# A two-layer encoder on one core: retention core interleaved with its out-projection, attention loop rebuilt, first norm as columns

## The reference, cut to what matters

```python
c_act = jax.nn.silu(c)
for i in range(DEPTH):                     # DEPTH = 2
    mod = c_act @ ada_w + ada_b            # 1024 x 6144
    sh1, sc1, g1, sh2, sc2, g2 = jnp.split(mod, 6, axis=-1)
    h = modulate(rmsnorm(x, n1), sh1, sc1) # h * (1 + scale) + shift
    m = retention_mixer(h, ...) if i == 0 else gqa_mixer(h, ...)
    x = x + g1[:, None, :] * m
    h = modulate(rmsnorm(x, n2), sh2, sc2)
    f = swiglu(h, ...) if i == 0 else moe_swiglu(h, ...)
    x = x + g2[:, None, :] * f
return modulate(rmsnorm(x, final_norm_g), fsh, fsc)

# retention: 4 heads, q and k 256 wide, v and gate 512 wide, w_in 1024 x 6144, w_out 2048 x 1024
y = (fwd + bwd)                            # decayed scores, forward and backward
y = ((y - mu) * lax.rsqrt(var + NORM_EPS)).reshape(bsz, seq, RET_V) * gn_g
return (jax.nn.silu(g) * y) @ w_out
# attention: 8 query heads, 2 key heads of 128, both RMS-normalised and rotated, softmax over 256 keys
# FFN: 2816 wide. Experts: 8, each 3584 wide, top 2 of 8 by token
```

## Time and profile before

| what | us |
|---|---|
| median of three executions | 1642.29 |
| profiled execution | 1642.87 |
| its span in the profile | 1641.0 |
| TensorE (PE) busy | 1545.9 |
| VectorE (DVE) busy | 1341.8 |
| ScalarE (ACT) busy | 976.7 |
| retention w_in, from unit 3 | 58.0 to 185.9 |
| retention core | 185.9 to 241.2 |
| its out-projection | 241.2 to 290.6 |
| FFN | 296 to 502 |
| QKV and attention | 509 to 620 |
| experts, last norm | 630 to the end |

### The profile page before, as it was taken

One profiled execution on the slowest core, in us unless ns is written; L12 is line 12 of the kernel. 1 busy time (PEld: TensorE's weight loads), 2 busy tenths in 40 slices (PEclk: granted clock), 3 DMA queues, 4 the chain that ended last, 5 costly groups with the idle time before them and its releaser, 6 DMA issues.

```text
span 1641.0 us, 20506 instructions
## 1 busy us (share of the span) xinstructions
PE 1545.9 (94%) x6782; PEld 1234.3 (75%) x6782; DVE 1341.8 (82%) x1047; ACT 976.7 (60%) x791; POOL 198.3 (12%) x189
## 2 busy tenths in 40 slices
PE   5999779899997779999999999999999999999996
PEld 4777547677776568888888888888888888888784
DVE  6799578877778668888888888888888888888897
ACT  3444523443334536677777677777777777777664
POOL 0399500000002001100100100000000000000600
PEclk8999979999998899999999999999999999999998
DMA  9799309688894417999999999999999999999992
GB/s 340 279 346 351 134 15 360 229 303 298 267 321 154 146 52 262 364 365 352 380 368 362 370 370 355 381 368 352 381 368 353 378 368 354 376 371 353 386 363 117
DMA packets 239918, 509.15 MB, mean 310 GB/s; under 512 B 16392, under 2 KB 39048, under 8 KB 239754
## 3 DMA queue, kind: packets, MB, share of 16 engines
q1 hardware_dynamic: 234704, 491.50, 83.0%
q0 software_dynamic: 4592, 15.08, 2.7%
q10 hardware_dynamic: 586, 2.11, 0.3%
HBM read 502.64 MB, written 7.87 MB: 311 GB/s over the span
## 4 chain that ended last, share of the span: by engine, by line
PE 89%; DVE 6%; ACT 1%; DMA 1%; issue 1%; SPq 0%; DVEq 0%; ACTq 0%
PE bank L1713 27%; PE bank L1714 27%; PE bank L1715 27%; PE bank L2045 1%; PE bank L1694 1%; PE bank L1803 1%; DVE lo L1096 1%; DMA xs<-in_x 1%; DMA stage<-in_l_moe_w_up 1%; PE bank L1708 1%; DVE hs L1134 0%; PE bank L1921 0%; DVE lo L1496 0%; SPq L453 0%; PE bank L2039 0%
## 5 line engine op out<-in xcount | busy, mean ns | idle before, releaser
L1496 DVE TENSOR_TENSOR lo<-stage,hi 128x2048 fp32r<-128x2048 f32 x168 | 386.3, 2306 | 52.4 <-ACT hi L958 51.8
L958 ACT CAST hi<-stage 128x2048 fp32r<-128x2048 f32 x168 | 321.4, 1913 | 118.2 <-DMA stage<-in_l_moe_w_up 94.2
L1714 PE MATMUL bank<-lo,hg_hi 128*128 128x512 f32 x896 | 354.6, 396 | 0.0
L677 ACT CAST hi<-stage 128x2048 fp32r<-128x2048 f32 x75 | 143.2, 1912 | 147.1 <-PE bank L1715 78.8
L1096 DVE TENSOR_TENSOR lo<-stage,hi 128x2048 fp32r<-128x2048 f32 x75 | 173.2, 2312 | 40.8 <-ACT hi L677 34.4
L1714 PEld LDWEIGHTS bank<-lo,hg_hi 128*128 128x128 f32 x896 | 168.9, 188 | 37.8
L1713 PE MATMUL bank<-hi,hT_hi 128*128 128x512 f32 x416 | 172.9, 416 | 9.9 <-DVE lo L1096 8.5
L1713 PE MATMUL bank<-hi,hg_hi 128*128 128x512 f32 x452 | 179.6, 397 | 1.4 <-DVE lo L1496 1.2
L1496 DVE TENSOR_TENSOR lo<-stage,hi_h 128x2048 fp32r<-128x2048 f32 x56 | 128.3, 2292 | 63.8 <-ACT hi_h L958 63.8
L1715 PE MATMUL bank<-hi,hg_lo 128*128 128x512 f32 x452 | 179.1, 396 | 0.0
L1714 PE MATMUL bank<-lo,eaT_hi 128*128 128x512 f32 x448 | 177.8, 397 | 0.0
(11 more groups left out here) (313 smaller groups left out, 2753.5 us busy)
## 6 DMA issues: line engine op xcount, KB each, us to landing
stage<-in_l_moe_w_gate SPq DMA_DIRECT2D x224, 512.0 KB, 4.6
stage<-in_l_moe_w_up SPq DMA_DIRECT2D x224, 512.0 KB, 5.2
stage<-in_l_moe_w_down SPq DMA_DIRECT2D x224, 512.0 KB, 4.8
ada_w<-in_l_ada_w SPq DMA_DIRECT2D x40, 1024.0 KB, 5.3
stage<-in_l_ret_w_in SPq DMA_DIRECT2D x48, 512.0 KB, 7.0
stage<-in_l_ffn_w_gate SPq DMA_DIRECT2D x22, 512.0 KB, 7.5
stage<-in_l_ffn_w_up SPq DMA_DIRECT2D x22, 512.0 KB, 8.6
stage<-in_l_ffn_w_down SPq DMA_DIRECT2D x22, 512.0 KB, 7.6
```

Of the source, the lines that this page charges most:

```text
L677: nc.scalar.copy(hi[:, b % HRING, :], stage[:, b % RING, :]).then_inc(hi_done, 1)
L958: nc.scalar.copy(hi_e(b), stage[:, b % RING, :]).then_inc(hi_done, 1)
L1496: nc.vector.tensor_tensor(lo[:, b % RING, :], stage[:, b % RING, :], hi_e(b).bitcast(F32), ALU.subtract).then_inc(lo_done, 1)
L1714: mm(dst_ap, a_hi, w_lo, start=False, stop=False)
```

## The change

It consists of three parts and a rotation of the cast buffers in the experts.

**First norm as columns.** c, the first norm's gain and the 2D bias values come packed as columns in one small DMA (`vecs`). x lands first; ScalarE scales it by the reciprocal root (`xr`), TensorE transposes it at once (`turn_x`, 16 transposes). `sum_pre` makes eight matmuls of one column, so shift and scale come out with channels on partitions; three small operations (`columns_pre`) finish them, and hT_hi, hT_lo are made per k of 128 channels (`high_pre`, `full_pre`, `low_pre`). The products of units 0 and 3 wait per k.

**Retention.** The decay arguments of all four heads are computed on VectorE at unit 8 of w_in, and the exponentials on ScalarE at unit 10. Ada halves 2 to 15 follow `low(u)` for u from 9 to 22 on VectorE; SyncE's text for w_in is unchanged. Gates go through Silu straight from PSUM. Head 0's transposes stand before the last unit of w_in. Heads and half units of the out-projection alternate; the out-projection's units come in another order, and so do the final ada halves.

**Attention.** The ada blocks leave it: `A_AT` is still loaded in the QKV projection but worked off, with `A_AT + 1`, in chunks 2 to 5 of the first expert. The rotation runs over two heads at a time; the transposes of the last queries, and their squares and roots, stand inside the head loop. The four output units are cast into other buffers (`high_o`).

Core of the diff:

```diff
-    sp.dma_start(ccol[:, :], c.rearrange("a (k p) -> p (a k)", p=P), allow_slow_non_contiguous=True).then_inc(c_in, 16)
+    sp.dma_start(vecs[:, :, :], columns.rearrange("p (a k) -> p a k", k=KT)).then_inc(c_in, 16)
+    xv = x.rearrange("a (t p) d -> p (a t) d", p=P)
+    for t in range(TT):
+        sp.dma_start(xs[:, t, :], xv[:, t, :]).then_inc(x_in[t], 16)
+    load_pre(0, 0)
     sp.dma_start(cst[:, 0:C_TRI], consts[:, 0:C_TRI]).then_inc(const_in, 16)
-    xv = x.rearrange("a (t p) d -> p (a t) d", p=P)
-    for k in range(KT):
+    for k in range(1, KT):
         load_pre(0, k)
-    sp.dma_start(xs[:, :, :], xv).then_inc(x_in, 16)
     load_in(0)
-    for u, ks in ((1, range(0, 4)), (2, range(4, 6)), (3, range(6, 8))):
+    load_in(1)
+    for u, ks in ((2, range(0, 2)), (3, range(2, 8))):
         for k in ks:
             load_pre(1, k)
         load_in(u)
...
         if 6 <= u < 6 + 2 * A_IN:
             a = u - 6
             load_ada(a // 2, a % 2, l0_ada_w, l0_ada_b, 2 * D + (a // 2) * AC)
-    for k in range(8):
-        n, kg = k // 4, k % 4
+    def load_out(k):
+        n, kg = OUT_ORDER[k]
         load(U_ROUT + k, w_out_v[:, 4 * kg:4 * kg + 4, n * CB:(n + 1) * CB])
-        load_ada(A_FIN + k // 2, k % 2, final_ada_w, final_ada_b, (k // 2) * AC)
...
+    def load_fin(i):
...
+        load_ada(A_FIN + i // 2, i % 2, final_ada_w, final_ada_b, (i // 2) * AC)
+    load_out(0)
+    load_fin(0)
+    load_out(1)
+    load_fin(1)
+    for k in range(2, 6):
+        load_out(k)
+    load_fin(2)
+    load_fin(3)
+    load_out(6)
+    load_fin(4)
+    load_out(7)
+    load_fin(5)
     load_pair(U_FF, 0, slice(0, FCH))
+    load_fin(6)
     load_pair(U_FF + 1, 4, slice(0, FCH))
+    load_fin(7)
...
+    chunks(0, 0, 1, 4)
+    load_ada(A_AT + 1, 0, l1_ada_w, l1_ada_b, (A_AT + 1 - A_L1) * AC)
+    chunks(0, 0, 4, 5)
+    load_ada(A_AT + 1, 1, l1_ada_w, l1_ada_b, (A_AT + 1 - A_L1) * AC)
+    chunks(0, 0, 5, N_EC)
...
     high_pre(1)
-    for u in range(5, 2 * N_IN + 3):
+    for u in range(4, 2 * N_IN + 1):
         cc = u // 2 - 2 if u >= 10 else u - 6
-        if u == 2 * N_IN + 2:
-            take_chunk(N_IN - 1)
         high(U_RET + u)
-        if 6 <= u < 9 or 10 <= u < 2 * N_IN + 2 and u % 2 == 0:
+        if 6 <= u < 9 or 10 <= u and u % 2 == 0:
             take_chunk(cc)
-        if u >= 11 and u % 2:
-            c = (u - 11) // 2
+        if u == 11:
+            ada_take(0, mod_at(2 * D))
+        if u >= 14 and u % 2 == 0:
+            c = (u - 12) // 2
             ada_take(c, mod_at(2 * D + c * AC))
...
+    qkv_copy(0)
+    qkv_squares(0)
+    high(U_QKV + 4)
     head_roots(0)
-    ada_take(A_AT, mod_at((A_AT - A_L1) * AC))
-    high(U_QKV + 4)
     high(U_QKV + 5)
-    qkv_take(1)
+    high_o(0)
+    high_o(1)
+    qkv_copy(1)
     aq_take(0)
-    high(U_AOUT)
+    qkv_squares(1)
+    aq_take(1)
+    act.wait_ge(w_used, RING + U_QKV + 4)
+    high_o(2)
     head_roots(1)
-    aq_take(1)
     aq_take(2)
-    high(U_AOUT + 1)
-    qkv_take(2)
-    head_roots(2)
     soft(0)
     soft(1)
-    aq_take(3)
-    aq_take(4)
+    act.wait_ge(w_used, RING + U_QKV + 5)
+    high_o(3)
+    qkv_copy(2)
     for h in range(AH):
         pT_take(h)
+        if h in (1, 3):
+            aq_take(3 + h // 2)
         if h:
             o_take(h - 1)
+        if h == 0:
+            qkv_squares(2)
+        if h == 1:
+            head_roots(2)
...
+    def columns_pre(half):
+        b, ks = COL_BANK[half], slice(AK * half, AK * half + AK)
+        dve.wait_ge(p_sum, half + 1)
+        nc.vector.tensor_tensor(pm[:, 0, ks], bank[:, b, 0:AK], vecs[:, 2, ks], ALU.add)
+        link(nc.vector.scalar_tensor_tensor(out=pm[:, 2, ks], in0=bank[:, b, AK:2 * AK], scalar=1.0,
+                                            in1=vecs[:, 3, ks], op0=ALU.add, op1=ALU.add))
+        nc.vector.tensor_tensor(pm[:, 1, ks], pm[:, 2, ks], vecs[:, 1, ks], ALU.mult).then_inc(p_col, 1)
+        dve.wait_ge(p_col, half + 1)
...
+        dve.wait_ge(xT_out, 4)
+        j = AK * half + k
+        link(nc.vector.tensor_scalar(yT[:, k, :], (xT0, xT1)[half][:, k, :], pm[:, 1, j:j + 1], pm[:, 0, j:j + 1], ALU.mult, ALU.add))
+    def low_pre(half, k):
+        j = AK * half + k
+        dve.wait_ge(h0_hi, j + 1)
+        nc.vector.tensor_tensor(hT_lo[:, j, :], yT[:, k, :], hT_hi[:, j, :].bitcast(F32),
...
-    low_pre(0)
+    pre(0, range(0, 1))
+    for t in range(TT):
+        dve.wait_ge(root_done, t + 1)
+        ins = nc.vector.reciprocal(rstd[:, t:t + 1], root[:, t:t + 1])
+        ins.then_inc(p_rstd, 1)
+    pre(0, range(1, KT))
+    columns_pre(0)
+    full_pre(0, 0)
+    full_pre(0, 1)
     low(U_RET)
-    pre(1, range(0, 4))
+    low_pre(0, 0)
+    low_pre(0, 1)
+    for k in (2, 3):
+        full_pre(0, k)
+        low_pre(0, k)
     low(U_RET + 1)
-    pre(1, range(4, 6))
+    pre(1, range(0, 2))
     low(U_RET + 2)
-    pre(1, range(6, 8))
-    low(U_RET + 3)
-    norm_pre(1)
-    low_pre(1)
-    low(U_RET + 4)
-    low(U_RET + 5)
+    pre(1, range(2, 8))
+    columns_pre(1)
+    for k in range(AK):
+        full_pre(1, k)
+        low_pre(1, k)
+    for u in range(3, 6):
+        low(U_RET + u)
...
     for u in range(6, 2 * N_IN):
         low(U_RET + u)
-        if u < 6 + 2 * A_IN:
-            ada((u - 6) // 2, u % 2)
...
+    weight(0)
+    stats(0)
+    weight(1)
+    gates(0)
+    stats(1)
+    low_y(0)
+    low_y(1)
+    weight(2)
+    gates(1)
+    stats(2)
+    low(U_ROUT + 2)
+    low_y(2)
+    low_y(3)
+    weight(3)
+    gates(2)
+    stats(3)
+    low_y(4)
+    low_y(5)
+    gates(3)
+    low(U_ROUT + 3)
+    fin(2)
+    low(U_ROUT + 4)
+    low_y(6)
+    low_y(7)
+    fin(3)
+    fin(4)
+    low(U_ROUT + 5)
+    fin(5)
...
-    link(head_rope(0))
...
     head_scales(0)
     kx = qkv[:, :, AH * AHD:(AH + AKV) * AHD].rearrange("p t (h d) -> p t h d", h=AKV)
...
-    low(U_QKV + 4)
     low(U_QKV + 5)
-    head_rope(1).then_inc(arope, 1)
+    head_rope(0, 2, qtab, 2 * TT).then_inc(arope, 1)
+    head_rope(2, 2, qtab, 2 * TT).then_inc(arope, 1)
     head_sums(1)
-    low(U_AOUT)
+    low_o(0)
     head_scales(1)
-    low(U_AOUT + 1)
...
+    for j in range(2, N_EC - 1):
+        b, i = U_MOE - 2 + 6 * j, 4 * (j - 2)
+        low_e(b)
+        ada_step(i)
+        e_mul(j - 1, RING + b - 2)
+        low_e(b + 1)
+        ada_step(i + 1)
+        low_e(b + 2)
+        low_e(b + 3)
+        ada_step(i + 2)
+        e_low_act(j - 1)
+        low_e(b + 4)
+        ada_step(i + 3)
+        low_e(b + 5)
...
+    keep_busy(8, 0)
+    turn_x()
+    keep_busy(24, 0)
+    sum_pre(0)
+    keep_busy(8, 0)
+    for u in range(2 * N_IN):
+        cc, kg = in_unit(u)
+        if kg == 0 and u >= 6:
+            pe.wait_ge(proj_out, cc + 1)
+        product(U_RET + u, 0, 4, 4 * kg, hT_hi, hT_lo, [bank[:, PAIRS[cc % 3][t], :] for t in range(TT)],
+                kg == 0, kg == 1, each=h0_done if u in (0, 3) else None, between=sum_second if u == 2 else None)
+        if u == 8:
+            ada_sum(0)
+        if u >= 11 and u % 2:
+            ada_sum((u - 9) // 2)
+        if u == 2 * N_IN - 2:
+            pe.wait_ge(rope_done, 1)
+            turn_qk(0, 7, 0)
     def scores(h):
...
     pe.wait_ge(proj_out, 3 + N_IN)
-    turn_qk(0)
-    for h in range(RH):
-        scores(h)
-        if h + 1 < RH:
-            turn_qk(h + 1)
...
-    OUT = [(0, 1), (6, 7)]
-    for k in range(8):
-        n, kg = k // 4, k % 4
-        product(U_ROUT + k, 0, 4, 4 * kg, yT_hi, yT_lo, [bank[:, OUT[n][t], :] for t in range(TT)],
-                kg == 0, kg == 3, tell=(k == 7))
-        if k in (2, 4, 6):
-            ada_sum(A_FIN + k // 2 - 1)
+    scores(0)
+    turn_qk(1, 4, 5)
+    values(0)
+    scores(1)
+    turn_qk(2, 4, 5)
+    values(1)
+    pe.wait_ge(kT_done, 3)
+    turn_y(0)
+    scores(2)
+    out_half(0, 0)
+    pe.wait_ge(yT_done, 2)
+    turn_qk(3, 4, 5)
+    values(2)
+    out_half(0, 1)
+    pe.wait_ge(kT_done, 4)
+    turn_y(1)
+    scores(3)
+    out_half(1, 0)
+    values(3)
+    turn_y(2)
...
         qkv_unit(k)
-    pe.wait_ge(arope, 1)
     aq_turn(0)
-    ada_sum(A_AT)
-    qkv_unit(4)
-    pe.wait_ge(arope, 2)
-    pe.wait_ge(a_out, 1 + A_AT + 1)
+    qkv_half(4, 0)
     aq_turn(1)
-    pe.wait_ge(aq_out, 1)
-    aq_turn(2)
-    qkv_unit(5)
-    pe.wait_ge(aq_out, 3)
+    qkv_half(4, 1)
+    pe.wait_ge(sq_done, 2 * TT)
+    pe.wait_ge(aq_out, 2)
     a_scores(0)
     a_scores(1)
-    pe.wait_ge(arope, 3)
-    aq_turn(3)
-    aq_turn(4)
+    aq_turn(2)
+    qkv_half(5, 0)
+    qkv_half(5, 1)
...
+    for j in range(2, N_EC - 1):
+        b = U_MOE - 2 + 6 * j
+        e_gate_up(b, 0, j)
+        if j == 4:
+            pe.wait_ge(put_done, 1)
+            ada_sum(A_AT)
+        if j == 5:
+            ada_sum(A_AT + 1)
+        e_down_step(b + 4, 0, j - 1, False, False)
+        e_turn(j)
```

621 lines of the change are left out of this document (337 added, 284 removed).

## The result

The changed kernel takes 1631.05 us (median of five executions, 1629.04 to 1631.97), the kernel before in the same series 1642.34 (1639.87 to 1645.94). The ratio is 0.9922 with a 95% interval of 0.991 to 0.9934, so 0.7% faster. The forecast was 1632. The profiled execution took 1629.04 us with a span of 1627.0, 14.0 less than before; it is the fastest of the five, and between the medians the difference is 11.3.

The account below looks back on a forecast made before the run. TensorE, busy for 94% of the span, bounds the kernel; only its waits and low clock can be won. A and B +12.5, C -16.6 +2.1, D -11.5, E -0.9, F +3.7 sum to -10.7: 1632 us, forecast 1624 to 1640, range 1613 to 1647.

Parts of the forecast that it names:

- B: w_in stage: unit loads wait for later ada steps, a turn spans two units, 15.5 us a pair; +16 us.
- C: Retention and out-projection: out-projection halves fill waits, -16.6 us; +2.1 us before the FFN's transposes.
- D: Attention: ada copy and sum gone, cast, rotation and transposes reordered; -11.5 us.
- A: First norm in columns: first product near 30.0, w_in unit 3 at 54.5 against 58.04; -3.5 us.
- R1: w_in: the loading chain does not bind, B is 0; about 1616 us, chance 0.14.
- The section's fit: w_in loads: 2.0 us fixed plus bytes at 436 GB/s, 6.8 us for ada half and unit; not used in the sum.
- R2: w_in: TensorE's clock falls through the stalled units, costing 22 us; about 1654 us, chance 0.12.
- R3: C and D overlap on paper only, each wins half: 1646, or 1641 if F's stall is nothing; chance 0.16.
- F: First expert: two ada sums +1.7 us, and 2 us of stall from VectorE's steps and memory traffic; +3.7 us.
- E: Router: one ada sum less behind the last transposes; -0.9 us.

Follow-up runs that it names:

- experiment 4: Kernel before with the first norm in column form alone: 1635.92 us, ratio 0.9957.
- experiments 1 and 2: Changed kernel, ada halves 2 to 15 loaded one unit later: 1605.84 us; kernel before, ada halves from the second on loaded one unit earlier: 1667.06 us.
- experiment 3: Changed kernel with the out-projection's half units taken out of the retention heads, all four heads first: 1639.33 us, ratio 0.9968.
- experiment 10: Kernel of experiment 8 with both last ada blocks back in the attention block, where the kernel before has them: 1616.29 us, ratio 0.9841.
- experiment 8: Kernel of experiment 7, one of two last ada blocks back in QKV, the other in first-expert chunks 2 and 3, loaded in attention: 1597.42 us, ratio 0.9722.
- experiment 7: Changed kernel with ada loads one unit later, plus head 0's transposes between the last w_in unit's token tiles: 1602.12 us, ratio 0.9753.
- experiment 6: Changed kernel without the loads of the last ada block, its steps, sums and copies kept: 1632.68 us, ratio 0.994.
- experiment 9: Kernel before with buffers 32 bytes lower: 1640.62 us, ratio 0.998; changed kernel with buffers 32 bytes higher: 1634.03 us, ratio 0.9947.

## Why the prediction came out right, point by point

**The total** was right to 1 us, and that is luck. B was 10 us too small, C and D together won 9 us more than forecast (37.3, not 28.1), and 3 us came from a source that was not in the sum; these errors cancelled.

**A** was right in kind. TensorE's first product starts at 28.27, not 30.0, and unit 3 1.9 us earlier than forecast. By itself it arrives whole at the end of w_in (experiment 4). The forecast let VectorE's step and not A set the end of w_in in this change, and that step came at 105.14 where 105.5 was forecast.

**B** was the step that mattered, and its mechanism is shown from both sides (experiments 1 and 2). The first stall came at 117.88 where 117.6 was forecast; rival R1 is out. The Trainium skill, page "DMA: Bandwidth & Descriptors", section "Anatomy of one DMA — SWDGE (gpsimd) path", puts the wait on the issuing sequencer, and the trace agrees: the load at 111.32 follows the step that ended at 111.24. That the loads queued behind it wait too is not in that sentence of the page; the rows of SyncE show it. The section's fit is for DMAs that GpSimd issues, and the estimate of 6.8 us for the two megabytes is too short for SyncE's queue here: from 111.32 to the cast at 119.15 are 7.8 and from 121.37 to the cast at 130.23 are 8.9. A pair of units took 15.9 us on average from unit 13 to unit 21, against 15.5. The term was mis-sized in its last three units. Unit 21 started at 181.34, 1.7 late; from there to the end took 25.0 us, not 18.8. VectorE's four ada steps took 6.05 us there and the next `lo` 3.12, while GpSimd multiplied the gates, and unit 23 waited 2.44 us for that `lo` (199.04) and then ran 1.5 us longer at low clock. Two of TensorE's sums (173.35 and 189.02) waited 1.36 and 1.81 us for ScalarE's ada copy, which now stands behind a cast and a Silu, the first time behind a table load of 1.28 us too. The forecast had looked at none of these for cost.

**R2** happened in part. The granted clock is 0.50, the lower level, from 117 to 123.7, from 151 to 154.4 and from 199 to 202.2 us, behind the waits of 3.83, 3.69 and 2.44 us; it stays at full behind those of 1.67, 1.72 and 1.29 us. The three spells put 6.6 us on TensorE's busy time (135.5 us in the stage against 127.8 before, of which 1.0 are the moved transposes). With the 18.2 us of idle time and the 1.0 they make up the stage's 25.9. The first two lie in pairs whose next unit still waited for `lo` (134.51 and 166.12), so there the chain set the pace; only the last spell's 1.5 us stand in the total.

**R3** did not happen: C and D together won more than forecast. Its second time is a slip of the sum: 1646 with F's 2 us of stall taken out is 1644, not 1641.

**C** had its parts right: 6.0 us of waits where 6.9 were forecast, and the 3 us for low clock were mostly not needed (1.00 in the core, 0.96 behind it). Experiment 3 confirms that filling gaps is the larger part.

**D** was right in direction and wrong in its reasons. I split 11.5 us over the rotation by pairs (-5.2), the cast (-3.3), a `low` (-2.7) and gave the ada work 2.3. With that work back at the places of experiment 10, the new order wins 1.0 us of 16.4. The step that failed is the reading of each wait by its last releaser, as in "after, that copy is gone and the cast stands before the key roots: -3.3". With the copy back and the cast ahead, the 4.80 us ahead of unit 4 come out as 6.47 one half unit later: the ada copy was the start of a delay that ran on through the block.

**E** was wrong in sign: the sum left, but half of the 32 router matmuls behind it started 0.21 us apart instead of 0.11, and gave it back. This is the clock: it is 0.50 from 612.0 to 615.2, where before it was 1.00 through all of them. With an ada sum ahead of them again, in experiment 8, they run at 1.00 and all 0.11 apart; without one, in experiment 7, half are at 0.21 as here. The forecast had counted a sum's time and not what the engine's work there does for its clock.

**F** was 1.2 too small. DMA was no part of it (experiment 6). The stall was 2.4 us where 2 were forecast, and the memory traffic that the forecast gave as one of its reasons was not the cause.

Of the signs that the prediction named, some did not come: w_in ended at 206.3 and not by 200, the core with the out-projection took 83.9 us and not 86 to 90, and two waits of the head loop are over 2 us (2.05 at 560.27, 2.10 at 566.44).

## What to carry to other kernels

In a queue that serves two streams, count for each load how many steps lie between the release it waits for and the step that needs what is behind it; an edit on another engine can shorten that distance without touching the queue, and moving one line of the queue gives it back. A total that comes out right tells little of its terms: time each stage against its forecast. A short wait or a removed piece of work can also change the clock of what follows, so read the granted clock of each stage beside its waits. Side work that only waits for slots belongs where no engine on the path queues behind it, and its price is that of the whole queue.

## What the runs showed of the hardware that was not expected

GpSimd and VectorE slow each other where they work at the same time. In the kernel before the rotation takes 105.6 us (69.75 to 175.4) with VectorE busy for 94.6 of them; in the changed kernel 86.3 us (64.5 to 150.8), with VectorE busy for 67.0. Rows of VectorE: four ada steps beside the rotation, with GpSimd idle, and beside the gate products, and the `lo` behind them.

```profile
107.68 3.56 DVE L1188 SCALAR_TENSOR_TENSOR ada_acc<-ada_w,cact,ada_acc 128x512 f32<-128x512 f32 x4
...
156.06 3.11 DVE L1188 SCALAR_TENSOR_TENSOR ada_acc<-ada_w,cact,ada_acc 128x512 f32<-128x512 f32 x4
...
189.66 6.05 DVE L1188 SCALAR_TENSOR_TENSOR ada_acc<-ada_w,cact,ada_acc 128x512 f32<-128x512 f32 x4
195.87 3.12 DVE L1176 TENSOR_TENSOR lo<-stage,hi 128x2048 fp32r<-128x2048 f32 x1 [0.15 <-DVE ada_acc L1188]
```

DMA is not the cause of the 6.05 us: from 202 to 206 us, where four steps took 3.11 again, DMA's share was 1.02. The gate products on GpSimd:

```profile
188.48 4.13 POOL L627 TENSOR_TENSOR proj<-proj,gn 128x512 f32<-128x512 f32 x2 [12.33 <-ACT proj L791]
...
193.88 2.97 POOL L627 TENSOR_TENSOR proj<-proj,gn 128x512 f32<-128x512 f32 x2 [1.27 <-ACT proj L791]
```

GpSimd's own steps in the rotation, first with VectorE idle (it waits until 115.34) and then beside the `lo` of 2.48 us that starts there:

```profile
112.89 0.47 POOL L604 TENSOR_TENSOR ropet<-proj,cst 128x128 f32<-128x128 f32 x1
...
115.63 2.51 POOL L604 TENSOR_TENSOR ropet<-proj,cst 128x128 f32<-128x128 f32 x1
```

The same operation of GpSimd takes 0.47 or 2.51 us, and the long one ends at 118.14, 0.32 us behind that `lo`.

The Trainium skill, page "SBUF — State Buffer", section "SBUF: two separate sides", names a port pair that the two share; an instruction of VectorE with two inputs from SBUF holds it to its end against a GpSimd instruction that reads SBUF, and the other is blocked for that time. The 2.51 us beside the `lo` agree with it; no run here takes the one engine's work away to test it.

The second is the 0.45 us of an expert pass that hang on 32 bytes of address (experiment 9).
